# The expert loop of a hierarchical MoE: column groups that divide output columns, and one transpose in place of four products

## The reference, cut to what matters

```python
g_w, g_i = lax.top_k(g_prob, 1)
...
e_w, e_i = lax.top_k(jax.nn.softmax(e_logits, axis=-1), TOP_K)
weights = e_w / jnp.sum(e_w, axis=-1, keepdims=True) * g_w
ids = g_i * EXPERTS_PER_GROUP + e_i
gates = jnp.sum(jax.nn.one_hot(ids, N_EXPERTS, dtype=jnp.float32) * weights[..., None], axis=1).astype(h.dtype)
hg = jnp.einsum('nd,edf->nef', t, w_gate)
hu = jnp.einsum('nd,edf->nef', t, w_up)
y = jnp.einsum('nef,efd->nd', jax.nn.silu(hg) * hu * gates[:, :, None], w_down)
```

## Time and profile before

| what | value |
|---|---|
| runs | 1391.13, 1392.63, 1405.95 us, median 1392.63 |
| the profiled execution | 1391.8 us, of it 1390.0 us span |
| granted clock of TensorE, mean | 0.933 of full speed |
| busy | PE 89%, its weight loads 51%, DVE 44%, ACT 20%, POOL 14% |
| chain that ended last | PE 83%, DVE 9%, "issue" 3% |
| read from HBM | 301.52 MB, 219 GB/s over the span |

### The profile page before, as it was taken

One profiled execution on the slowest core, in us unless ns is written; L12 is line 12 of the kernel. 1 busy time (PEld: TensorE's weight loads), 2 busy tenths in 40 slices (PEclk: granted clock), 3 DMA queues, 4 the chain that ended last, 5 costly groups with the idle time before them and its releaser, 6 DMA issues.

```text
span 1390.0 us, 26450 instructions
## 1 busy us (share of the span) xinstructions
PE 1242.8 (89%) x9235; PEld 715.7 (51%) x9236; DVE 605.2 (44%) x1303; ACT 273.2 (20%) x672; POOL 200.4 (14%) x249
## 2 busy tenths in 40 slices
PE   4899849988978889999989999999996999999996
PEld 3554435655455445555555565343545544555553
DVE  0121453345234334444454433588644233444445
ACT  1111323333010111211223212221011111122111
POOL 1021240000010112222210000111000022221231
PEclk9799968999977999999999999999995998999998
DMA  9542168785252298999993231100028069996794
GB/s 324 189 151 88 61 236 288 247 301 187 83 243 121 91 364 359 407 418 393 400 348 124 73 92 60 61 0 0 1 88 358 0 276 419 382 378 270 295 423 173
DMA packets 80145, 304.79 MB, mean 219 GB/s; under 512 B 10872, under 2 KB 11809, under 8 KB 54729
## 3 DMA queue, kind: packets, MB, share of 16 engines
q1 hardware_dynamic: 77098, 298.66, 55.6%
q10 hardware_dynamic: 2752, 4.53, 0.9%
q0 software_dynamic: 224, 0.61, 0.1%
HBM read 301.52 MB, written 2.24 MB: 219 GB/s over the span
## 4 chain that ended last, share of the span: by engine, by line
PE 83%; DVE 9%; issue 3%; ACT 2%; DMA 1%; SPq 1%; POOL 1%; POOLq 0%; DVEq 0%; ACTq 0%
PE banks L427 80%; DVE arena L950 4%; DMA arena<-in_ada_b 1%; DVE arena L1086 1%; PE banks L591 1%; ACT arena L1541 1%; SPq L1816 1%; POOL arena L1717 1%; PE banks L478 1%; SPq L1814 0%; DVE arena L1096 0%; DVE arena L961 0%; PE banks L791 0%; DVE arena L1084 0%; DVE arena L995 0%
## 5 line engine op out<-in xcount | busy, mean ns | idle before, releaser
L427 PE MATMUL banks<-arena 32*128 32x256 f32 (+12 forms) x8904 | 1196.2, 424 | 83.1 <-issue 17.6
L427 PEld LDWEIGHTS banks<-arena 128*32 128x32 f32 (+5 forms) x8904 | 675.2, 156 | 568.9 <-issue 411.1
L950 DVE TENSOR_TENSOR arena<-banks,arena 128x64 f32<-128x64 f32 (+4 forms) x284 | 113.9, 412 | 109.1 <-PE banks L427 74.6
L950 DVE TENSOR_TENSOR arena<-arena 128x384 f32<-128x384 f32 (+11 forms) x229 | 156.3, 688 | 4.4
L1205 DVE SCALAR_TENSOR_TENSOR arena<-arena 128x768 f32<-128x768 f32 x81 | 83.0, 1024 | 92.7 <-issue 88.5
L1742 POOL COPY arena<-arena 128x256 f32 x79 | 64.1, 812 | 287.5 <-PE banks L427 157.2
L1578 ACT ACTIVATE arena<-banks 128x512 f32<-128x512 f32 x79 | 47.2, 597 | 252.6 <-PE banks L427 252.6
L1215 DVE TENSOR_SCALAR arena<-arena 128x64 f32<-128x64 f32 x79 | 15.4, 195 | 182.0 <-ACT arena L1582 182.0
L1733 POOL TENSOR_TENSOR arena<-arena 128x256 f32<-128x256 f32 x81 | 59.7, 737 | 225.2 <-PE banks L427 225.2
L1716 POOL TENSOR_SCALAR arena<-arena 128x8 f32<-128x8 f32 (+2 forms) x28 | 10.4, 371 | 423.3 <-ACT arena L1438 294.2
L1304 DVE TENSOR_SCALAR arena<-arena 128x385 f32<-128x385 f32 x24 | 11.5, 481 | 82.5 <-ACT arena L1639 82.5
(11 more groups left out here) (144 smaller groups left out, 450.4 us busy)
## 6 DMA issues: line engine op xcount, KB each, us to landing
arena<-in_moe_w_gate SPq DMA_DIRECT2D x64, 1024.0 KB, 8.2
arena<-in_moe_w_up SPq DMA_DIRECT2D x64, 1024.0 KB, 10.2
arena<-in_moe_w_down SPq DMA_DIRECT2D x64, 1024.0 KB, 10.5
arena<-in_ada_w SPq DMA_DIRECT2D x24, 2048.0 KB
arena<-in_hy_w_in SPq DMA_DIRECT2D x6, 2048.0 KB
arena<-in_attn_w_in SPq DMA_DIRECT2D x3, 2048.0 KB
arena<-mod_rows SPq DMA_DIRECT2D x8, 512.0 KB, 9.8
arena<-in_attn_w_out SPq DMA_DIRECT2D x2, 2048.0 KB
```

The costliest lines, as they stand in the source:

```text
L427: return pe.matmul(out, lhsT, rhs, start=start, stop=stop, skip_group_check=True)
L950: return dve.tensor_tensor(o, p, q, op)
```

## The change

`hidden` now gives each of the four column groups a quarter of the output columns in place of a quarter of the channels. Group q takes output columns 128 q to 128 q + 127 of the 512 for all eight channels: 32 products of 32x128 in place of eight of 32x512. The bank `pg` then holds finished sums, 128 columns of it. ACT copies those 128 columns. `summed` is one transpose of the 128x128 tile. The down weights are permuted on the host, since the hidden units come out in another order; each partition's run in memory stays as long. SP's first three loads of the Hyena mixer wait for every expert slot that their memory touches.

```diff
--- before.py
+++ after.py
@@ -367,7 +367,7 @@
         rw = v(WORK + 6832, 768)
         iota = v(WORK + 7600, 768)
         xcur = v(WORK + 8368, KC, M)
-        gsb = v(WORK + 8624, 2, P, 2)
+        gsb = v(WORK + 8624, P)
         ysb, yprev = v(WORK + 6832, DE), v(WORK + 7088, DE)
         posr, wr, parts = (v(HTO + 768 * i, 2, NTOK) for i in range(3))
         share, share_last = v(HTO + 2304, NTOK), v(HTO + 2304 + NTOK, NTOK)
@@ -681,8 +681,9 @@
                     gu = expert(slot)[0]
                     pe.wait_ge(s_["moe_x"], g + 1)
                     for k in range(KC):
-                        c = slice(32 * (k % 4), 32 * (k % 4) + 32)
-                        last = mm(pg[c, :].rearrange("p (i n) -> p i n", i=2), xcur[:, k, :], gu[:, :, k, :], k < 4, k >= 4)
+                        for q in range(4):
+                            last = mm(pg[32 * q:32 * q + 32, 0:P], xcur[:, k, :], gu[:, q // 2, k, (q % 2) * P:(q % 2 + 1) * P],
+                                      k == 0, k == KC - 1)
                     last.then_inc(s_["moe_pg"], 1)
 
                 def down_product(g, slot):
@@ -712,9 +713,7 @@
                 def summed(g):
                     pe.wait_ge(s_["moe_g"], g + 1)
                     pe.wait_ge(s_["moe_y"], g + 1)
-                    for c in range(4):
-                        last = mm(pt[:, c * M:(c + 1) * M], gsb[:, c // 2, :, c % 2], sel)
-                    last.then_inc(s_["moe_pt"], 1)
+                    pe.transpose(pt[:, 0:P], gsb, ident).then_inc(s_["moe_pt"], 1)
 
                 def one_step(g, slot, before):
                     hidden(g, slot)
@@ -1575,7 +1574,7 @@
 
                 def gates(g):
                     act.wait_ge(s_["moe_pg"], g + 2)
-                    act.activation(gsb.rearrange("p i q f -> p (i q f)"), pg, ACT.Copy).then_inc(s_["moe_g"], 1)
+                    act.activation(gsb, pg[:, 0:P], ACT.Copy).then_inc(s_["moe_g"], 1)
 
                 def sigmoid(g):
                     act.wait_ge(s_["moe_pt"], g + 1)
@@ -1929,8 +1928,10 @@
                 for i, src in enumerate((a["hy_filt_b1"][0], a["hy_filt_freq"][0, 0], a["hy_filt_b2"][0], a["hy_filt_freq"][0, 1])):
                     for half in range(1 if i < 2 else 2):
                         sp.dma_start(fcol[half * FF:(half + 1) * FF, i:i + 1], src.rearrange("(p o) -> p o", o=1)).then_inc(in_hy, 16)
-                for i, k in enumerate(items1[:3]):
-                    sp.wait_ge(down_free[i], NE // 4)
+                for k in items1[:3]:
+                    o = number[k] % 3 * MSLOT
+                    for s in range(o // ESLOT, (o + MSLOT - 1) // ESLOT + 1):
+                        sp.wait_ge(down_free[s], NE // 4)
                     load(k)
                 sp.wait_ge(down_free[3], NE // 4)
                 for c, (nme, n) in enumerate((("hy_b_in", 24), ("hy_conv_b", 24))):
@@ -1996,6 +1997,8 @@
     zt, win = filter_positions()
     for n in ("attn_w_in", "hy_w_in", "moe_w_group", "moe_w_router", "moe_w_gate", "moe_w_up"):
         arrays[f"in_{n}"] = channel_rows(arrays[f"in_{n}"])
+    w = arrays["in_moe_w_down"]
+    arrays["in_moe_w_down"] = np.ascontiguousarray(np.swapaxes(w.reshape(2, NE, 2, P, D), 2, 3)).reshape(w.shape)
     arrays["in_bias"] = bias_windows(arrays.pop("in_na_rpb"))
     arrays.update(in_tab=table(), in_dft=dft_table(), in_zt=zt, in_win=win)
     a = {k[3:]: nc.dram_tensor(k, v.shape, F32, kind="ExternalInput").ap() for k, v in arrays.items()}
```

## The result

The changed kernel takes 1527.3 us in the median (four runs, 1519.5 to 1535.3) against 1395.05 us of the kernel before (four runs, 1391.1 to 1406.0). The ratio is 1.0935, its interval 1.0849 to 1.1020: 9% slower. The forecast was 1447 us with a range of 1380 to 1512, so the direction was right and the time lies outside the range, 15 us over its upper end.

The account below looks back on a forecast made before the run. The prediction took PE's expert steps as the bound, with the register reads as a step's second limit. Its terms summed as 1391.8 - 12 + 2 + 20 + 45 = 1446.8 us, range 1380 to 1512.

Parts of the forecast that it names:

- the register reads: PE's reads of the next expert's two registers, behind most steps: they end within 0.7 us of the next step.
- Rival D: Expert steps: the register reads do not hold the next step, so every step gains 0.8 us; 1372 us, chance 0.10.
- SP's longer wait: SP's three Hyena loads wait for more slots, about 6 us extra, but covered: 0 us, +6 without cover.
- Step 1: The sum in each expert step: one transpose for four products saves 0.8 us in 15 steps without register reads, -12 us.
- Step 2: `hidden` in each expert step: 64 records of 128 columns for 16 of 512 cost +0.02 us in 79 steps, +2 us.
- Step 4, first passes: First pass through each layer's expert loop: ten more code blocks to fetch at 1.0 to 1.4 us, +20 us.
- The bound of 60: Worst case for the loops' first passes: 2.2 us more on each of some 28 blocks from shorter head start.
- rival B: Expert loop's later passes: every code block is kept, no second fetch; 1402 us, 1390 to 1430, chance 0.27.
- Step 4, later passes: Layer 0's expert loop: nine blocks don't fit, so six jumps back wait 7.5 us each for code, +45 us.
- only the block at the loop's top is lost: The forecast's own case for layer 0's jumps back: one block lost; 1447 us, 1410 to 1500, chance 0.35.
- rival C: Layer 0's loop: all blocks are read again each pass, 17.3 us a pass, 104 for six; 1506 us, chance 0.20.

Follow-up runs that it names:

- k1_fit: The changed kernel with never-executed products ahead of each layer's expert steps, so that both layers' loops lie over seven code blocks; 1411.1 us.
- k3_grown: The kernel before, its own products kept, with never-executed products added so that its loop touches eight blocks in layer 0 and seven in layer 1; 1587.3 us.
- k10_light_after: The changed kernel with transfers of expert weights behind the first four experts cut to an eighth in bytes; 1474.2 us.
- k2_out: The changed kernel with never-executed products ahead of layer 1's steps alone, so that layer 1's loop also lies over eight blocks; 1633.2 us.

## Why the prediction was wrong

**What bounds the kernel, and the reads.** Right. PE was the bound, ACT and POOL stayed hidden, and the register reads were the second limit of a step: the steps with reads took 5.8 to 6.0 us and those without fell to 5.14 (5.1 was forecast). Rival D (chance 0.10) fell; the experiment with early reads shows what it would have needed. SP's longer wait didn't show: from the last step of layer 0 to the first of layer 1 (ACT's copies) it is 407.4 us before, 411.4 after and 406.6 in k1_fit, and 417.7 in k3_grown, which has the old waits.

**Step 1, -12 us.** Right. In layer 1 32 steps gave 10.1 us: nine of them are second steps and gave 0.77 each, 6.9, as forecast; the other 3.2 came from steps with reads, which the forecast had at nothing. In layer 0 the stalls hide it; in k1_fit 25 steps gave 25 x 6.07 - 148.24 = 3.5 us.

**Step 2, +2 us.** 0.03 us a step alone, 79 x 0.03 = 2.4.

**Step 4, first passes, +20 us.** Too small: they are 33 us in k1_fit, where nothing is read twice (11.6 in the first ten steps of layer 0 and 21.5 in the first seven of layer 1). The share of one block, 1.0 to 1.4 us in the old code, isn't a constant: over k1_fit's own steady steps it is 2.0 us for layer 0's 13 blocks (84.97 - 10 x 148.24/25) and 2.7 for layer 1's 11 (70.30 - 7 x 186.24/32). The bound of 60 had this in it, by the shorter head start of 3.5 us; the value taken did not. That rival B's sum (10 us over the kernel before) lies near k1_fit's 13.3 is in part luck, since step 1 gave more as well.

**Step 4, later passes, +45 us: this step failed.** It asked the right question (do nine blocks stay?) and found the right layer. Its price of a jump back, 7.5 us, is near the 5.6 to 8.2 of the six, but partly by luck: it was taken from how long the weights take to land, and k10_light_after shows 4.5 to 5.5 us of it beside an eighth of the weights, whose transfers land in 2.3 to 3.3 us there (medians). It failed in the rule by which blocks give way. I took the case in which only the block at the loop's top is lost, with chance 0.35, over the one in which each fetched block evicts the one needed next, rival C with 0.20. The packets decide: 54 are read again, nine a pass, so every block is, and the later passes cost 116 us (1527.3 against 1411.1 in k1_fit) in place of 45. I had no row for the first rule. For the second there was an argument that I wrote down myself (code is passed in order, so the block needed next is the oldest) and then gave the lower chance. The Trainium skill (Runtime: NRT & Kernel Launch, Instruction fetch mechanics) calls the buffer a FIFO of 2048 instructions in blocks of 256; on both counts the runs agree: 7 + 1 blocks stay, 8 + 1 don't, and all go together. A buffer that gave up the block used longest ago would look the same in these loops. The page's sentence on a window of only two blocks doesn't hold here, as the old loop had shown already.

**Rival C's own sum** was 1506 us. It is 21 short: 116/6 = 19.4 us a pass were measured and 17.3 forecast, 12 us in all; the first passes are 13 short, and step 1 gave back some. With the measured pieces the sum closes: 1391.8 - 10.1 - 3.5 + 33 + 116 = 1527. Within a pass C lacked the jumps forward (up to 3.5 us each), the waits in straight code (4.49 us, where it had 1.4 a block) and the clock, which fell to 0.81 in the stretch of stalls and made PE's own work 21.5 us longer in 25 steps. I had named the clock for `hidden` in the first passes and not here.

**The range** ended at 1512, 6 us over C's centre, and left out C's upper half. With C at 0.20 and its terms uncertain by more than 6 us, it should have reached further.

## What to carry to other kernels

Count instructions, not only what they do. A change that replaces a few wide products by many narrow ones can leave an engine's busy time as it is or better and still lose, if the loop's body, skipped branches included, outgrows the engine's code buffer; before such a change, divide the loop's instructions by the 256 of a packet, count the blocks that it touches where it lies, add the block ahead, and expect all of them again in each pass if the sum is over eight. Register reads behind a step's last product are a hidden floor: put them ahead of a wait that the sequencer has to sit through anyway (20 us here).

## What the runs showed of the hardware

- PE keeps eight blocks of 16.5 KB (256 instructions), the one fetched ahead among them. A loop over seven is never read again (62 packets), one over eight is read whole in every pass (nine packets each), in either layer (115 and 169 packets). By the count 36 instructions are the slack: the loop is 6.86 blocks long. The shifts tried were of some 100 and more.
- A jump back to an evicted block held PE's sequencer for 5.6 to 8.2 us in the changed kernel, for 3.4 to 8.7 us in k2_out, and for 4.5 to 5.5 us in layer 0 beside an eighth of the weights. From its first packet to the end of the jump it was 4.0 to 4.2 us both beside the full weights' stream and beside an eighth of it; what the stream added was the time before that packet. With one packet alone (two jumps of k2_out) the whole jump took 3.4 and 3.9 us.
- A jump forward to code that isn't there waits as well: up to 3.5 us where it skipped 210 instructions and up to 6.7 where it skipped some 290. So does straight code: 4.49 us in the middle of `hidden`.
- The stalls took the granted clock from 0.99 to 0.81 over 240 us; part of a stall's price falls on the products behind it.
